# Two reduced-precision products for the decay exponents of a state-space scan, with GpSimd making one operand

## The reference, cut to what matters

```python
def segsum(a):
    T = a.shape[-1]
    a_rep = jnp.broadcast_to(a[..., None], a.shape + (T,))
    a_rep = jnp.where(jnp.tril(jnp.ones((T, T), bool), -1), a_rep, 0.0)
    s = jnp.cumsum(a_rep, axis=-2)
    return jnp.where(jnp.tril(jnp.ones((T, T), bool)), s, -jnp.inf)

def ssd(x, dt, a, bm, cm, h0, chunk):
    ...
    da = dt_h * a.astype(jnp.float32)[None, :, None, None]
    da_cs = jnp.cumsum(da, axis=-1)
    m = jnp.einsum('bclhn,bcshn->bhcls', cm, bm) * jnp.exp(segsum(da)) * dt_h[:, :, :, None, :]
    y_diag = jnp.einsum('bhcls,bcshp->bclhp', m, x)
    w_end = jnp.exp(da_cs[..., -1:] - da_cs) * dt_h
    states = jnp.einsum('bclhn,bhcl,bclhp->bchpn', bm, w_end, x)
    ...
    y_off = jnp.einsum('bclhn,bchpn,bhcl->bclhp', cm, new_states[:, :-1], jnp.exp(da_cs))
    return (y_diag + y_off).reshape(Bsz, L, H, P), new_states[:, -1]
```

## Time and profile before

| | us |
|---|---|
| three runs | 1404.17, 1400.85, 1400.43 (median 1400.85) |
| the profiled execution | 1398.23 |
| its span, first to last instruction | 1396.5 |
| PE busy in the span | 1301.9 (93%) |
| DVE, ACT, POOL busy | 862.4, 623.7, 203.3 |
| mean granted TensorE clock | 0.966 of 2.4 GHz |

### The profile page before, as it was taken

One profiled execution on the slowest core, in us unless ns is written; L12 is line 12 of the kernel. 1 busy time (PEld: TensorE's weight loads), 2 busy tenths in 40 slices (PEclk: granted clock), 3 DMA queues, 4 the chain that ended last, 5 costly groups with the idle time before them and its releaser, 6 DMA issues.

```text
span 1396.5 us, 22313 instructions
## 1 busy us (share of the span) xinstructions
PE 1301.9 (93%) x8147; PEld 1063.8 (76%) x8147; DVE 862.4 (62%) x1300; ACT 623.7 (45%) x881; POOL 203.3 (15%) x277
## 2 busy tenths in 40 slices
PE   5999999889889998999699996999999999997996
PEld 4887999678757676767578864888888888874885
DVE  4422555377745454555545556988888888855663
ACT  4324224423122222222423225788888888855332
POOL 1110000123122222231001002000000000003541
PEclk9999999999789999999899998999999999998998
DMA  7316111135379999992565537698666999984551
GB/s 263 122 58 155 54 46 34 36 146 169 115 234 328 339 309 341 306 334 96 178 243 196 211 136 268 243 336 315 233 235 239 333 397 398 397 331 158 193 191 61
DMA packets 140926, 306.40 MB, mean 219 GB/s; under 512 B 23441, under 2 KB 57874, under 8 KB 140482
## 3 DMA queue, kind: packets, MB, share of 16 engines
q1 hardware_dynamic: 119730, 229.82, 47.3%
q0 software_dynamic: 14976, 54.53, 10.9%
q10 hardware_dynamic: 6096, 20.45, 4.0%
HBM read 251.27 MB, written 53.49 MB: 218 GB/s over the span
## 4 chain that ended last, share of the span: by engine, by line
PE 45%; DVE 2%; DMA 2%; issue 1%; ACT 1%; POOL 0%; POOLq 0%; SPq 0%; ACTq 0%; DVEq 0%
PE pb L2262 6%; PE pb L2264 6%; PE pb L2263 6%; PE pb L2286 3%; PE pb L2288 3%; PE pb L2287 3%; PE pb L2578 2%; PE pb L2579 2%; PE pb L2580 2%; PE pb L1776 2%; PE pb L1778 2%; PE pb L1777 2%; PE pb L2247 1%; PE pb L1800 1%; PE pb L1688 1%
## 5 line engine op out<-in xcount | busy, mean ns | idle before, releaser
L1459 ACT ACTIVATE prob<-pb,nmx 128x1024 f32<-128x1024 f32 (+3 forms) x64 | 47.5, 741 | 172.8 <-DVE nmx L1504 172.8
L2441 DVE TENSOR_TENSOR low_gate<-raw_gate,high_gate 128x2048 fp32r<-128x2048 f32 x44 | 99.2, 2289 | 25.4 <-ACT high_gate L2345 25.4
L2441 DVE TENSOR_TENSOR low_down<-raw_down,high_down 128x2048 fp32r<-128x2048 f32 x44 | 98.9, 2288 | 17.8 <-ACT high_down L2345 17.8
L2441 DVE TENSOR_TENSOR low_up<-raw_up,high_up 128x2048 fp32r<-128x2048 f32 x44 | 98.9, 2288 | 4.3 <-ACT high_up L2345 2.1
L2345 ACT CAST high_gate<-raw_gate 128x2048 fp32r<-128x2048 f32 x44 | 82.1, 1907 | 5.6 <-SPq L2186 3.1
L516 PE MATMUL pb<-hH,blkH 128*128 128x344 f32 x264 | 84.5, 320 | 0.0
L517 PE MATMUL pb<-hL,blkH 128*128 128x344 f32 x264 | 84.3, 319 | 0.0
L518 PE MATMUL pb<-hH,blkL 128*128 128x344 f32 x264 | 84.3, 319 | 0.0
L1274 POOL DMA_INDIRECT rows<-in_cache_r,pt_at x64 | 60.6, 947 | 159.4 <-PE pb L1385 140.9
L2345 ACT CAST high_up<-raw_up 128x2048 fp32r<-128x2048 f32 x44 | 82.3, 1918 | 1.7 <-SPq L2186 1.4
L2345 ACT CAST high_down<-raw_down 128x2048 fp32r<-128x2048 f32 x44 | 82.0, 1910 | 0.3 <-issue 0.2
(11 more groups left out here) (430 smaller groups left out, 3271.6 us busy)
## 6 DMA issues: line engine op xcount, KB each, us to landing
colsA<-in_cache_t SPq DMA_DIRECT2D x256, 144.0 KB
raw_gate<-in_w_gate SPq DMA_DIRECT2D x32, 1024.0 KB, 9.3
raw_up<-in_w_up SPq DMA_DIRECT2D x32, 1024.0 KB, 9.4
raw_down<-in_w_down SPq DMA_DIRECT2D x32, 1024.0 KB, 8.8
y_d<-yo ACTq DMA_DIRECT2D x22, 512.0 KB, 6.4
y_d<-zero SPq DMA_DIRECT2D x16, 512.0 KB
raw<-in_w_blk SPq DMA_DIRECT2D x15, 512.0 KB, 3.6
xt<-in_x_all SPq DMA_DIRECT2D x9, 512.0 KB, 5.2
```

Source lines behind the costliest of these rows:

```text
L2441: dve.tensor_tensor(part(low_[w], c), part(raw[w], c), part(high[w], c).bitcast(F32), ALU.subtract).then_inc(S(w + "_low"), 1)
```

## The change

The step sizes `da` of all 64 pairs of chunk and head are split once into a high part rounded to fp32r (`daH`) and the rest (`daL`), by two DVE instructions of 64 columns ahead of the first triangle. DVE makes the triangle of the high part as before (`rdaH`, now fp32r). POOL makes that of the low part (`rdaL`, 128 x 1024) in a new step `low_steps`. PE takes, for each half of the heads, two fp32r products (`rdaH`, then `rdaL`) into one PSUM bank where it took one fp32 product, and waits for both triangles. `rdaL` lies in the bytes of `shist`, so the load of `shist` moves from before the loop to SP's step 6, behind a wait for the last triangle product. Several semaphores of the attention block are merged into `prep_dve` and `row_max`, each wait turned into a count on the merged one.

```diff
-        strict = sb_in(p1, "strict", [P, P])
+        strict = sb_in(p1, "strict", [P, P], F32R)
...
+        rdaL, = stretch(0, ("rdaL", [P, H, P], F32R))
         shist = sb_in(p1c, "shist", [P, NB * INNER])
...
-        rda = sb_in(p1d, "rda", [P, H, P])
+        rdaH = sb_in(p1d, "rdaH", [P, H, P], F32R)
...
+        daH, daL = [sb_in(p1d, n, [P, PT * H], F32R) for n in ("daH", "daL")]
...
             load_z(0)
             load_z(1)
-            sp.dma_start(shist[:, :], ssm_prev).then_inc(S("shist_in"), 16)
...
                 if j == 3:
                     first_heads()
+                if j == 6:
+                    sp.wait_ge(S("dec_mm"), PT)
+                    sp.dma_start(shist[:, :], ssm_prev).then_inc(S("shist_in"), 16)
...
                 pe.wait_ge(S("rda_rdy"), j + 1)
+                pe.wait_ge(S("rdaL_rdy"), j + 1)
...
                 for half in range(2):
-                    last = pe.matmul(pb[:, 2 + half, :], strict[:, :], rda[:, 4 * half:4 * half + 4, :].rearrange("p h l -> p (h l)"), start=True, stop=True)
+                    of = lambda r: r[:, 4 * half:4 * half + 4, :].rearrange("p h l -> p (h l)")
+                    pe.matmul(pb[:, 2 + half, :], strict[:, :], of(rdaH), start=True, stop=False)
+                    last = pe.matmul(pb[:, 2 + half, :], strict[:, :], of(rdaL), start=False, stop=True)
                 last.then_inc(S("dec_mm"), 1)
...
+            def low_steps(j):
+                if j:
+                    pool.wait_ge(S("dec_mm"), j)
+                else:
+                    pool.wait_ge(S("da_rdy"), 3)
+                pool.tensor_tensor(rdaL[:, :, :], bc(daL[:, j * H:(j + 1) * H].bitcast(F32), 2, [P, H, P]), bc(tri, 1, [P, H, P]), ALU.mult).then_inc(S("rdaL_rdy"), 1)
+
+            low_steps(0)
             rows(0)
             skip(0)
+            low_steps(1)
             for j in range(PT):
                 if j + 1 < PT:
                     rows(j + 1)
                     skip(j + 1)
+                if j + 2 < PT:
+                    low_steps(j + 2)
                 inverse_root(sty[:, j % 2, :], "y", j)
...
+                    flat = da[:, 0:PT, :].rearrange("p t h -> p (t h)")
                     dve.wait_ge(S("chunk_mm"), NC * (CT + 3))
                     dve.wait_ge(S("da_rdy"), 1)
-                dve.tensor_tensor(rda[:, :, :], bc(da[:, j, :], 2, [P, H, P]), bc(tri, 1, [P, H, P]), ALU.mult).then_inc(S("rda_rdy"), 1)
+                    dve.tensor_copy(daH[:, :], flat).then_inc(S("da_rdy"), 1)
+                    dve.wait_ge(S("da_rdy"), 2)
+                    dve.tensor_tensor(daL[:, :], flat, daH[:, :].bitcast(F32), ALU.subtract).then_inc(S("da_rdy"), 1)
+                dve.tensor_tensor(rdaH[:, :, :], bc(daH[:, j * H:(j + 1) * H].bitcast(F32), 2, [P, H, P]), bc(tri, 1, [P, H, P]), ALU.mult).then_inc(S("rda_rdy"), 1)
...
-            pool.wait_ge(S("pt_at_rdy"), 1)
+            pool.wait_ge(S("prep_dve"), prepared("page_rows"))
...
-                dve.wait_ge(S("masked"), t + 1)
+                dve.wait_ge(S("row_max"), 2 * t + 1)
```

More of the change, by code:

```diff
@@ L1214, in program @@
         DVE_STEPS = ["largest", "new", "copied", "new_largest", "joined", "by_head", "scaled", "bound", "sum", "probs", "inverse", "values", "latent"]
+        PREP_STEPS = ["zero_row", "pad", "zero_qr", "zero_sum", "table", "scaled", "page_rows", "swapped", "ropes", "latents", "new"]
+        prepared = lambda what: PREP_STEPS.index(what) + 1
         LINKS = ["bounds", "spread", "turned"]
@@ L1288, in _ @@
                 if b == 0:
-                    pool.wait_ge(S("qr_rdy"), 1)
-                    pool.wait_ge(S("qlat_rdy"), 1)
+                    pool.wait_ge(S("prep_dve"), prepared("ropes"))
+                    pool.wait_ge(S("prep_dve"), prepared("latents"))
                 else:
@@ L1343, in latent_queries @@
                 last.then_inc(S("prep_pe"), 1)
-                pe.wait_ge(S("pad_rdy"), 1)
+                pe.wait_ge(S("prep_dve"), prepared("pad"))
                 for c in range(2):
@@ L1358, in page_scores @@
                     else:
-                        pe.wait_ge(S("newT_rdy"), 1)
+                        pe.wait_ge(S("prep_dve"), prepared("new"))
                 pages = cols_of[q % 3]
@@ L1497, in bounds @@
                 dve.wait_ge(S("sc_mm"), t + 1)
-                dve.tensor_tensor(diag, diag, cst[:, CS_CAUS:CS_CAUS + P], ALU.add).then_inc(S("masked"), 1)
-                dve.wait_ge(S("masked"), t + 1)
-                dve.tensor_reduce(mx[:, t % 2:t % 2 + 1], sc(t)[:, 0:(i + 1) * P], AX.X, ALU.max).then_inc(S("mx_rdy"), 1)
-                dve.wait_ge(S("mx_rdy"), t + 1)
+                dve.tensor_tensor(diag, diag, cst[:, CS_CAUS:CS_CAUS + P], ALU.add).then_inc(S("row_max"), 1)
+                dve.wait_ge(S("row_max"), 2 * t + 1)
+                dve.tensor_reduce(mx[:, t % 2:t % 2 + 1], sc(t)[:, 0:(i + 1) * P], AX.X, ALU.max).then_inc(S("row_max"), 1)
+                dve.wait_ge(S("row_max"), 2 * t + 2)
                 if t >= 2:
@@ L1523, in fill @@
             def fill():
[L1526 to L1529, removed]
-                dve.wait_ge(S("pt_in"), 32)
[L1531 to L1535, removed]
+                ready = S("prep_dve")
+                dve.memset(att_rows[:, PT, :], 0.0).then_inc(ready, 1)
+                dve.memset(pb[:, 7, :], 0.0).then_inc(ready, 1)
+                dve.memset(qr4[:, :, :, :], 0.0).then_inc(ready, 1)
+                dve.memset(rs[:, :], 0.0).then_inc(ready, 1)
+                dve.wait_ge(S("pt_in"), 32)
+                dve.tensor_copy(pt_f[:, 0, :], pt_rows[:, :]).then_inc(ready, 1)
+                dve.wait_ge(ready, prepared("table"))
+                dve.tensor_scalar(pt_f[:, 1, :], pt_f[:, 0, :], 32.0, None, ALU.mult).then_inc(ready, 1)
+                dve.wait_ge(ready, prepared("scaled"))
+                dve.tensor_tensor(pt_at[:, :], pt_f[:, 1, :], cst[:, CS_ROW32:CS_ROW32 + 1].broadcast_to([P, NB * 8]), ALU.add).then_inc(ready, 1)
             def queries():
+                ready = S("prep_dve")
                 dve.wait_ge(S("qT_rdy"), H)
-                dve.tensor_copy(qsw[NOPE:QD, :, :], qT[QD:, :, :]).then_inc(S("fill_dve"), 1)
-                dve.wait_ge(S("fill_dve"), 5)
+                dve.tensor_copy(qsw[NOPE:QD, :, :], qT[QD:, :, :]).then_inc(ready, 1)
+                dve.wait_ge(ready, prepared("swapped"))
                 for m in range(4):
@@ L1543, in queries @@
                                              qsw[NOPE:QD, :, :].rearrange("p h t -> p t h"), ALU.add)
-                last.then_inc(S("qr_rdy"), 1)
+                last.then_inc(ready, 1)
                 dve.wait_ge(S("prep_pe"), 1)
-                dve.tensor_copy(qlat[:, :, :, :], pb[:, 6, 0:2 * H * NB].rearrange("p (c h b) -> p c b h", c=2, h=H)).then_inc(S("qlat_rdy"), 1)
+                dve.tensor_copy(qlat[:, :, :, :], pb[:, 6, 0:2 * H * NB].rearrange("p (c h b) -> p c b h", c=2, h=H)).then_inc(ready, 1)
                 dve.wait_ge(S("prep_pe"), 2)
-                dve.tensor_copy(newT[:, :, :], pb[:, 7, 0:3 * P].rearrange("p (c t) -> p c t", c=3)).then_inc(S("newT_rdy"), 1)
+                dve.tensor_copy(newT[:, :, :], pb[:, 7, 0:3 * P].rearrange("p (c t) -> p c t", c=3)).then_inc(ready, 1)
             did = S("paged_dve")
@@ L1559, in paged @@
                     if b == 0:
-                        dve.wait_ge(S("fill_dve"), 2)
+                        dve.wait_ge(S("prep_dve"), prepared("zero_sum"))
                     dve.tensor_reduce(smx[:, 0:1], pb[:, 6, 0:2 * P], AX.X, ALU.max).then_inc(did, 1)
@@ L1608, in _ @@
             dve.wait_ge(S("prep_pe"), 3)
-            dve.wait_ge(S("att_zero"), 1)
+            dve.wait_ge(S("prep_dve"), prepared("zero_row"))
             dve.tensor_copy(att_rows[0:NB, PT, :], pb[0:NB, 6, :]).then_inc(S("att_dec"), 1)
```

## The result

| | before | after |
|---|---|---|
| median of six runs each, us | 1402.28 (1397.86 to 1407.3) | 1417.19 (1409.22 to 1424.3) |
| the profiled execution, us | 1398.23 | 1419.93 |
| its span, us | 1396.5 | 1418.2 |
| mean granted TensorE clock | 0.966 | 0.953 |
| POOL busy, us | 203.3 | 219.3 |

The kernel after is slower: the ratio is 1.0117, interval 1.0091 to 1.0143, which on 1402.28 is 16.4 us (12.8 to 20.1). The forecast was 8.1 us. The direction was right, and the time lies inside the range, near its upper end, but half of the loss stands in no term of the sum.

What follows compares the result with a forecast made beforehand. The prediction took PE to bound the chunk loop. It added 6.2 us for the loop and 1.9 for the stage's start, 8.1 together, to 1400.85, giving 1409.0 us, with a range from 1402.5 to 1418.

Steps and rivals of the forecast that it cites:

- PE bounds the loop: Chunk stage: PE busy for all of 11 us, DVE for 8.82, POOL for 3.95; chunks start 10.80 us apart.
- six waits: Chunks 2 to 7: PE waits 1.90 us each for POOL's low triangle, which stands behind xskip.
- The low triangle: One POOL instruction over 128 x 1024 elements, priced at 1.91 us, between 0.95 and 3.1.
- The period without a fall: Time from one chunk's decay products to the next: 11.83 us in place of 10.80.
- This part of the sum: Loop, chunks 2 to 7: 1.90 us of wait less 0.87 of product, 1.03 more six times, 6.2 us.
- an estimate of 2.2 us: POOL's low triangle at the skill page's 2.6 cycles an element and 1.2 GHz; it would make the time 1411.
- DVE and POOL blocked each other at the start: Start of the stage: POOL's second triangle and DVE take turns ahead of the first wqL, costing 1.9 us.
- the first query product: Start of the stage: PE's first query product, at 283.72 before, expected near 285.6.
- the rows: Trace rows used for POOL's price: 1.68 ns an element, nearer to 2.0 cycles, kept over the page's 2.6.
- Four products: PE's four fp32r decay products per chunk, 0.23 us apart: 0.92 us where two fp32 products take 1.79.
- The moved load: Load of shist in SP's step 6: taken as nothing, with 0.6 us as the upper end.
- The forecast's own count: Load of shist: 8.8 us to landing, so at 371.2 at the latest, with its first user starting at 370.58.

Runs made afterwards that it cites:

- e5: The kernel after with two low-triangle buffers, POOL one chunk further ahead, and the load of shist at the head of SP's step 6: 1398.5 us, ratio to before 0.9997.
- e8: Rerun beside the kernel before of the kernel after with ACT making the low triangle and shist loaded at the head of SP's step 6: 1395.41 us, ratio 0.997.
- e2: The kernel after, with PE taking high products first, repeated three times from chunk 2 on, and only low products waiting: 1406.58 us, ratio to before 1.0052.
- e3: The kernel after with the load of shist moved to the head of SP's step 6, ahead of the stores: 1417.79 us, ratio to before 1.0138.
- e1: The kernel after, but POOL makes the low triangle for chunk 0 only and all chunks use it: 1396.22 us, ratio to before 0.9984.
- e6: The kernel before with only the change's merged semaphores of the attention block (prep_dve, row_max): 1398.68 us, ratio to before 1.0011.
- e7: The kernel before, unchanged, run once more for a second profile: 1403.04 us in its one execution.

## Why the prediction gave half of the loss

**Right.** PE bounds the loop, and GpSimd's place in its own order turns the saving into a wait: six waits of 1.84 us for a forecast of 1.90, ended by POOL. The low triangle took 1.89 (forecast 1.91). The period without a fall is 11.9 (11.83). This part of the sum, 6.2 us, was 6.6, and e5, which moves nothing but POOL's work (with a second buffer for it) and the load, shows that the place is the cause: the same instruction one chunk ahead costs the loop nothing. The Trainium skill's "GPSIMD Engine Reference", section "Performance versus the Vector engine", led to an estimate of 2.2 us; the measured 1.89 decides for the rows.

**Right in kind, smaller in size.** DVE and POOL blocked each other at the start as forecast, with the first query product at 285.54 (forecast 285.6), of which 1.4 us belong to the change, not 1.9; that the time itself came out so near is luck, since the stage began 0.46 later in this execution. Four products took 1.02, not 0.92: the first distance among them is 0.31, not 0.23, and the forecast carried a distance from the middle of a run of products to its head.

**Wrong: a term taken as nothing.** The moved load was costed at nothing, with an upper end of 0.6; it made DVE wait 1.03. The forecast's own count gave 0.6 and was set aside with the reason that the load would have less beside it in its new place; it took 8.8 us from issue to landing as before, and the count was the better guide.

**Open.** In chunk 0 the clock stays low longer in the kernel after (0.50 from 270.8 to 294.7) and in e5 (273.4 to 293.9) than in e8 (from 273.7 to 287.4), although PE waits about 5 us for `wqL` in all of them. In the four profiles with a triangle of POOL's behind the first `xskip` (after, e2, e3, e5) the clock rises 8 to 10 us behind the first query product, in the six without one 3 to 4 us behind it. e1, which differs there from the kernel after by this triangle alone, is among the six. So the loss comes with the blocked start; but each of these is a single execution, and which of the pauses does it was not tried. In e6 and e7, which have the chunk stage of before, chunk 0 takes 9.7 us, not 9.2, so the change costs 2.5 to 3.0 us there.

## What to carry to other kernels

Where one engine is the bound and never pauses, price a new pause of it twice: its length, and the products behind it at the lower clock level; if the trace of before shows one pause with a fall behind it, that is the row to go by. Ask of work that goes to an idle engine not how much idle time that has but what it stands behind in that engine's order: the same instruction of 1.89 us stands behind a loss of 1.2% in the kernel after and, with one chunk of lead, behind none in e5. If a wait can't be moved, splitting it so that only the last operand waits gives back part of it (0.5 us per chunk in e2), and work without use in the gap kept the clock there.
